# Compact copies of the second half's weights, and a new order of steps at the opening of the first attention

## The reference

```python
def first_block(...):            # two layers; what the change touches is in layer 0
    cq, ckv, kr = z[..., :256], z[..., 256:384], z[..., 384:416]      # z = h @ w_in
    q  = (rmsnorm(cq, q_norm_g) @ w_uq).reshape(b, t, 8, 96)
    kv = (rmsnorm(ckv, kv_norm_g) @ w_ukv).reshape(b, t, 8, 128)
    # q and k normed per head, rotated; softmax attention; retention beside it; @ w_out
    # modulation: 6 chunks per layer of silu(c) @ ada_w + ada_b

def second_block(...):
    x = x + hybrid_mixer(rmsnorm_2(x), w_in, ..., w_out)              # w_in_2: 1024 x 3080
    x = x + memory_cross_attention(rmsnorm_2(x), rmsnorm_2(mem), wq, wkv, wo)
    x = x + peer_ffn(rmsnorm_2(x), wq, subkeys, u_tab, v_tab)
    # peer_ffn: per token 8 heads x 16 experts; rows u_tab[i], v_tab[i] of 1024 floats
    # act = gelu(u_tab[i] . x) * gate;  out = sum act * v_tab[i]
    return rmsnorm_2(x, norm_final_w)
```

## Time and profile before

| | us |
|---|---|
| median of 3 runs | 4487.05 |
| lowest and highest run | 4479.52, 4492.16 |
| profiled execution | 4478.17 |
| its span, first to last instruction | 4476.4 |
| PE busy / DVE busy / POOL busy / ACT busy | 3652.3 / 2022.0 / 1399.2 / 1008.0 |
| bytes moved by DMA | 821.56 MB |

### The profile page before, as it was taken

The page is one execution under the profiler, slowest core; times in us unless marked ns, Lnnn a source line. Parts: engine busy times, 40 slices in busy tenths (PEclk is TensorE's granted clock), DMA queues, the critical chain, the costliest instruction groups (busy, mean ns, idle before and its releaser), DMA issues.

```text
span 4476.4 us, 45304 instructions
## 1 busy us (share of the span) xinstructions
PE 3652.3 (82%) x16837; PEld 2077.9 (46%) x16837; DVE 2022.0 (45%) x4634; ACT 1008.0 (23%) x2265; POOL 1399.2 (31%) x1494
## 2 busy tenths in 40 slices
PE   6788998999999778999997979867777776565555
PEld 3355534555555565444466867434544433111111
DVE  2565062633222583111125324586755655665553
ACT  3564022200000211100025122344132212112111
POOL 0000001162422000000000002656556677776776
PEclk8899999999999899999998989888888888776667
DMA  4232102222222123422211134988889999998998
GB/s 176 76 113 81 57 23 49 76 108 95 76 82 112 64 112 123 153 76 75 75 66 71 57 132 161 351 319 309 284 296 368 346 392 334 350 353 326 354 354 318
DMA packets 287765, 821.56 MB, mean 184 GB/s; under 512 B 24040, under 2 KB 60340, under 8 KB 284244
## 3 DMA queue, kind: packets, MB, share of 16 engines
q0 software_dynamic: 150832, 565.17, 34.2%
q1 hardware_dynamic: 136320, 253.22, 15.9%
q10 hardware_dynamic: 420, 0.62, 0.1%
HBM read 791.67 MB, written 27.26 MB: 183 GB/s over the span
## 4 chain that ended last, share of the span: by engine, by line
PE 57%; DVE 13%; POOL 8%; issue 8%; ACT 5%; DMA 4%; another core or an unknown queue 3%; SPq 0%; DVEq 0%; ACTq 0%; POOLq 0%
PE bank L722 25%; PE bank L2619 6%; PE bank L2855 5%; POOL arena L1170 4%; POOL ring L1161 4%; PE bank L2422 3%; PE bank L2579 2%; PE bank L2474 2%; DVE ring L2279 2%; DMA arena<-in_peer_v,arena 2%; PE bank L2338 1%; PE bank L587 1%; PE bank L2414 1%; PE bank L2559 1%
## 5 line engine op out<-in xcount | busy, mean ns | idle before, releaser
L1161 POOL DMA_INDIRECT ring<-in_peer_u,arena x512 | 569.3, 1112 | 1412.5 <-DVE arena L2226 1071.9
L2855 PE MATMUL bank<-arena 64*64 64x512 f32 x4096 | 697.8, 773 | 375.1 <-issue 311.9
L2279 DVE SCALAR_TENSOR_TENSOR ring<-ring,xT 128x1024 f32<-128x1024 f32 x512 | 614.2, 1222 | 265.7 <-DMA ring<-in_peer_u,arena 244.1
L1170 POOL DMA_INDIRECT arena<-in_peer_v,arena x512 | 579.5, 1132 | 206.2 <-issue 145.1
L722 PE MATMUL bank<-hT,ring 128*128 128x512 f32 (+1 forms) x1536 | 553.3, 522 | 5.1 <-ACT hT L637 5.1
L2855 PEld LDWEIGHTS bank<-arena 64*64 64x64 f32 x4096 | 187.8, 162 | 793.7 <-issue 790.9
L722 PE MATMUL bank<-arena,ring 128*128 128x512 f32 (+1 forms) x1536 | 551.3, 521 | 0.0
L722 PEld LDWEIGHTS bank<-hT,ring 128*128 128x128 f32 x1536 | 292.6, 191 | 264.1 <-issue 250.9
L722 PEld LDWEIGHTS bank<-arena,ring 128*128 128x128 f32 x1536 | 291.8, 190 | 258.1 <-issue 244.2
L2619 PE MATMUL bank<-hT,ring 128*128 128x256 f32 x1536 | 366.7, 398 | 33.6 <-DMA ring<-in_peer_wq 15.6
L2619 PEld LDWEIGHTS bank<-hT,ring 128*128 128x128 f32 x1536 | 302.6, 200 | 125.5 <-issue 54.1
(11 more groups left out here) (520 smaller groups left out, 4581.2 us busy)
## 6 DMA issues: line engine op xcount, KB each, us to landing
ring<-in_mlp_w SPq DMA_DIRECT2D x32, 2048.0 KB, 8.3
ring<-in_ada_w SPq DMA_DIRECT2D x24, 2048.0 KB, 13.0
s_store<-arena POOLq DMA_DIRECT2D x8, 2816.0 KB, 9.6
ring<-in_w_in SPq DMA_DIRECT2D x10, 2048.0 KB, 8.1
arena<-s_store SPq DMA_DIRECT2D x16, 1024.0 KB, 6.9
ring<-in_w_in SPq DMA_DIRECT2D x12, 1024.0 KB
ring<-in_w_out SPq DMA_DIRECT2D x4, 2048.0 KB, 8.0
ring<-in_s_w_glu SPq DMA_DIRECT2D x4, 2048.0 KB, 14.2
```

Source lines behind the costliest of these rows:

```text
L1161: pool.indirect_dma_start(u_row[k % ERING], None, I["peer_u_2"][0], bass.IndirectOffsetOnAxis(idxs[:, k // EXPERTS, k % EXPERTS:k % EXPERT ...
L1170: pool.indirect_dma_start(v_row[v % ERING], None, I["peer_v_2"][0], bass.IndirectOffsetOnAxis(idxs[:, v // EXPERTS, v % EXPERTS:v % EXPERT ...
L2279: dve.scalar_tensor_tensor(row, row, 1.0, h_tok[k // EXPERTS % 2], ALU.mult, ALU.mult, accum_out=dots[k // AGROUP % 2][:, k % AGROUP:k % A ...
L2855: last = pe.matmul(banks[2 * r + n][QUADS[r if y == 0 else 1 - r], :], diag[QUADS[r], s, :], v_row[s][QUADS[r], 512 * n:512 * n + 512], st ...
```

## The change

Three things:

- During the first attention's end, behind the retention blocks, SP issues 32 copies from the weight inputs to a new scratch tensor `weights_kept` in device memory. Each copy takes the 256 columns that one block of the second half needs, so that a partition's share of a block lies in one piece of 8 KB. The second half's loads (`mix1`, `w2_1`, `xq1`, `wo1`, `pq1`) read from there (`kept_blocks`), after a wait of SP for all copies. The first half's loads stay.
- The opening computes z in the order keys, queries 0, queries 1, rotary part. The sums of the key norm come behind queries 0. ACT and DVE follow the same order.
- The six modulation units of the first attention each come one head earlier: the first before head 0's rotation.

```diff
@@ mla_order
     yield "proj", 0
-    for step in ("nsum", "norm", "rot"):
-        for j in range(2):
+    for step in ("nsum", "ada", "norm", "rot"):
+        for j in range(1 if step == "ada" else 2):
             yield step, j
+    yield "adarow", 0
     for n in range(6 * H_A + 3):
         if n < 6 * H_A:
             yield "scores", n
+        if n == 0:
+            yield "adacol", 0
...
-        if h <= ADA_IN_MLA and n % 6 in (2, 3, 4):
-            yield ("ada", "adarow", "adacol")[n % 6 - 2], h - 1
+        if h < ADA_IN_MLA and n % 6 in (2, 3, 4):
+            yield ("ada", "adarow", "adacol")[n % 6 - 2], h
+
+MLA_IN_ORDER = (("z_kv", 2), ("z_q0", 0), ("z_q1", 1), ("z_kr", 3))
@@ build
+        TAIL_WEIGHTS = [*[("w_in_2", (2056, 2568, 0, 512, 1024, 1536)[j // 2] + 256 * (j % 2)) for j in range(12)],
+                        *[(name, 256 * j) for name, n in (("w_out_2", 4), ("xattn_wq_2", 4), ("xattn_wo_2", 4), ("peer_wq_2", 8)) for j in range(n)]]
+        tail_at = {"mix1": 0, "w2_1": 12, "xq1": 16, "wo1": 20, "pq1": 24}
+        weights_kept = nc.dram_tensor("weights_kept", (len(TAIL_WEIGHTS), P, KD * 256), F32).ap()
@@ SP
             for j in range(4):
                 load_block(sp, block0["w_in_r"] + j, w_in_v[:, :, MLA_IN + j * RET_W:MLA_IN + (j + 1) * RET_W])
+            for b, (name, a) in enumerate(TAIL_WEIGHTS):
+                sp.dma_start(weights_kept[b].rearrange("p (k n) -> p k n", k=KD),
+                             I[name][0].rearrange("(k p) n -> p k n", p=P)[:, :, a:a + 256]).then_inc(S("weights_kept"), 16)
             for j in range(2):
                 load_block(sp, block0["w_out"] + j, ...)
...
+            def kept_blocks(name, lo, hi):
+                for j in range(lo, hi):
+                    load_block(sp, block0[name] + j, weights_kept[tail_at[name] + j])
...
-            mix_blocks(1, 0, 3)
+            sp.wait_ge(S("weights_kept"), 16 * len(TAIL_WEIGHTS))
+            kept_blocks("mix1", 0, 3)
...
-            tail_blocks(1, "w2_1", "w_out_2", 256)
-            tail_blocks(1, "xq1", "xattn_wq_2", 256)
+            kept_blocks("w2_1", 0, 4)
+            kept_blocks("xq1", 0, 4)
@@ ACT (DVE and PE likewise)
-            for m in range(4):
+            for name, m in MLA_IN_ORDER:
...
+                if name == "z_q0":
+                    norm_roots(act, "ckv", TBS, KV_LORA, rs=rstd_qk[:, 0, :])
             norm_roots(act, "cq", TBS, Q_LORA)
-            norm_roots(act, "ckv", TBS, KV_LORA, rs=rstd_qk[:, 0, :])
```

More of the change, by code:

```diff
@@ L300 @@
     ("ada_first1", 2),
-    ("z_q", 4), ("z_kv", 2), ("z_kr", 2),
-    ("norm_cq", 2), ("norm_ckv", 2),
+    ("z_kv", 2), ("z_q0", 2), ("norm_ckv", 2),
+    ("z_q1", 2), ("z_kr", 2), ("norm_cq", 2),
     ("v_tok", 6),
@@ L1003, in _, with mix_blocks @@
             MIX_AT = (2056, 2568, 0, 512, 1024, 1536)
-            def mix_blocks(h, lo, hi):
+            def mix_blocks(lo, hi):
                 for j in range(lo, hi):
-                    a, n = (MIX_AT[j], 512) if h == 0 else (MIX_AT[j // 2] + 256 * (j % 2), 256)
-                    load_block(sp, block0[f"mix{h}"] + j, w_in2[:, :, a:a + n])
+                    load_block(sp, block0["mix0"] + j, w_in2[:, :, MIX_AT[j]:MIX_AT[j] + 512])
+            def kept_blocks(name, lo, hi):
+                for j in range(lo, hi):
+                    load_block(sp, block0[name] + j, weights_kept[tail_at[name] + j])
             def mask_loads(h):
@@ L1012, in mask_loads, with tail_blocks @@
                     sp.dma_start(mask(h, j), cst(name)).then_inc(S("g_masks"), 16)
-            def tail_blocks(h, name, src, width, lo=0, hi=None):
+            def tail_blocks(name, src, lo=0, hi=None):
                 w = I[src][0].rearrange("(k p) n -> p k n", p=P)
[L1016 to L1020, removed]
+                for j in range(lo, hi or w.shape[2] // 512):
+                    load_block(sp, block0[name] + j, w[:, :, j * 512:(j + 1) * 512])
+            mix_blocks(0, 2)
+            mix_blocks(2, 3)
             for n in range(8):
@@ L1023, in _ @@
             mask_loads(0)
-            mix_blocks(0, 3, 6)
-            tail_blocks(0, "xkv", "xattn_wkv_2", 512)
-            tail_blocks(0, "w2_0", "w_out_2", 512)
+            mix_blocks(3, 6)
+            tail_blocks("xkv", "xattn_wkv_2")
+            tail_blocks("w2_0", "w_out_2")
             for n in range(8):
@@ L1054, in _ @@
             sp.dma_start(ring[:, 3, :], kv_kept).then_inc(S("kv_moved"), 16)
-            tail_blocks(1, "wo1", "xattn_wo_2", 256)
+            kept_blocks("wo1", 0, 4)
             for n in range(8):
                 filled(sp, ticket0[f"xout1_{n}"])
-            tail_blocks(1, "pq1", "peer_wq_2", 256)
+            kept_blocks("pq1", 0, 8)
             for T_ in range(NTL):
@@ L1200, in _ @@
             norm_shift(act, "l0a", TBS, hT, shift_of(0, 0))
-            for m in range(4):
+            for name, m in MLA_IN_ORDER:
                 for b, (lo, hi) in enumerate(TBS):
-                    t = ticket0["z_q"] + 2 * m + b
+                    t = ticket0[name] + b
                     bank = filled(act, t)
@@ L2339, in _ @@
                     fill(last, t)
+                if name == "z_q0":
+                    norm_sums(pe, "ckv", TBS, prob, 1, per=2)
             norm_sums(pe, "cq", TBS, sqs, 2, per=2)
-            norm_sums(pe, "ckv", TBS, prob, 1, per=2)
             wv = block(pe, block0["ukv"], 1, n=1024)[:, 0, :].rearrange("p (h two v) -> p h two v", h=H_A, two=2)
```

14 lines of the change are left out of this document (7 added, 7 removed).

## The result

The changed kernel took **4439.52 us** (median of 4 runs, 4435.46 to 4445.42) against 4483.28 us for the kernel before (4 runs, 4478.08 to 4492.16): ratio 0.9903, 95% interval 0.9885 to 0.9922. The forecast was 4,449 us with a range of 4,412 to 4,480, and "faster" at 0.74. One execution of e3 took 5627.97 us and is left out of its ratio; the other eleven took 4482.46 to 4495.70.

A forecast was written before the change was run, and what follows sets the result against it. PE was taken to set the pace for 25 of 40 slices, then the gather stage with DMA 80 to 100% busy. Terms -12.6 - 0.4 - 0 - 25 = -38 us from 4,487.05 gave 4,449 us, range 4,412 to 4,480.

The forecast's parts named there:

- 1. Opening order: First attention's opening: `v_tok` starts without a wait at 99.97, first attention product at about 107.9 instead of 120.48; -12.6 us.
- It moves as a whole: Everything behind the first attention product is a chain through ACT and DVE that moves earlier with it, by 12.6 us.
- 2. Modulation unit: First attention: the 3.63 us unit fits PE's 8.71 us wait behind head 0's sums; taken as -0.4 us.
- 3. The copies: SP's queue from 365 us: 32 copies done by 573, before `w_out` is needed at 704; cost 0.
- 4. The loads: Second half beside the gathers: 8 KB rows land a block in about 5.5 us instead of 16; -25 us.
- The others vanish: PE's block waits in the second half: longest, 15.6 us, shrinks by about 10.5; those of 6.7, 6.3, 4.2 vanish.
- term 1: The new order of z products and norms in the first attention's opening, put at -12.6 us.
- What is next late: Gather stage, once weight loads land sooner: the DVE product on its gather is the next to be late.
- A: Gather stage is limited by bytes, large rows don't help, only the opening counts: 4,474 us; chance 0.22.
- D: Second half: large rows hold up gathers, 32 blocks each stalling the ticks by 3 us: 4,542 us; chance 0.05.
- C: Copies run into retention and delay `w_out`; at 80 GB/s it is 97 us late: 4,546 us; chance 0.06.
- B: The mixed stage's whole chain speeds up as sooner landings free the next slots; -55, 4,419 us; chance 0.15.

The follow-up runs named there:

- e3: Kernel before plus the 32 copies, which nobody reads; second half's loads still in 1 KB rows, old order: 4487.9 us, ratio 1.0001 to the kernel before.
- e7: Kernel before with only the new order of z products and norms; modulation units at old places, no copies: 4477.34 us, ratio 0.9971.
- e1: Changed kernel without the copies and with the old 1 KB row loads, so only the new opening and modulation order: 4476.03 us, ratio 0.9972.
- e10: The changed kernel once more, unaltered, with more runs, against the kernel before: 4434.07 us, ratio 0.9907.
- e8: Kernel before with only the modulation units moved to their new places: 4471.6 us, ratio 0.9996.
- e9: Whole change with every copy made four times (128 copies), against the kernel before: 4453.57 us, ratio 1.0178.
- e2: Kernel before plus the copies and the second half's loads in 8 KB rows, opening and modulation in old order: 4465.75 us, ratio 0.9955.
- e6: Kernel before without copies, old order, second half's blocks read in 8 KB rows from the u table: 4361.16 us, ratio 0.9952.
- e4: Whole change with the compact 1 MB blocks stored and read in 1 KB rows, against the kernel before: ratio 0.9984.
- e5: Whole change with each block in 4 KB rows (two pieces, 64 copies of 512 KB), against the kernel before: ratio 0.9928.

## Why the prediction was right

*1. Opening order (-12.6).* Right, in place and size. `v_tok` began at 99.32 (said: 99.97), the first attention product at 107.39 (said: 107.9), 13.1 us earlier; e7 measured -13.0 and e1 -12.6 us at the end. "It moves as a whole" held from there to the rotation (-12.0) and to `w_out` (706.88 against 717.48: -10.6; e10 has 705.79 and e1 703.91, e7 705.47).

*2. Modulation unit (-0.4).* Right within what can be measured: e8 -1.8 us, interval -7.6 to +4.5. The gap closed as worked out, 8.71 = 3.63 + 5.10 to 0.02 us.

*3. The copies (0).* Right: e3 1.0001. The time at which `w_out` is needed was read from the long row (704 instead of 682), which cost nothing here. The rate was mis-sized, on the safe side. I took the 161 GB/s of a spill and an end by 573 us; SP's next load was issued at 472.54, and with a landing of 13.1 us, the median of the last copies in the page, they were through by some 485 us, where the DMA share falls from 1.01 to 0.17 (from 480 to 485 us and from 485 to 490): 33.6 MB in 120 us, 280 GB/s. In e9, 134.2 MB in 434 us make 309 GB/s.
The Trainium skill (DMA: Bandwidth & Descriptors, Latency and other measured facts) gives 207 GB/s for copies at a 512 KiB pitch, by which, an estimate, they would have lasted 162 us. These copies, whose source rows are 1 KB long, were faster than that; the measurement decides.

*4. The loads (-25).* Right in kind, its size in the middle of what was measured: -20 in the old order (e2, e6), -29 to -30 on top of the new opening (e1 to the whole). Three steps in it were off. The landing of a block was put at 5.5 us where the earlier trace rows had 16 to 18; the kept blocks in the chains took 4.8 to 8.8 us, with a median of 8.4 in e9. "The others vanish" failed in one place: two waits stayed, 6.1 us before the mixer's product at 2817.98 and 6.6 before the `peer_wq` products at 3548.73, 12.7 in all where I had left 5. And I counted the waits as the trace of before had them, 32.8 us (34.6 with one of 1.8 that I hadn't counted), though term 1 moves the whole stage and one wait was short by luck of its place. That makes up for the two steps before it, so that the size of the term came out this near is in part luck. The sum of -38 stood against -43.5 and -41.6.

Of the signs named, the idle time by DMA fell to 12.7 us in the profiled execution and to 8.7 in e10 (said: under 10). The stage from 2,770 to 3,660 us was said to be 25 us shorter; it was 12.8 us shorter between the two traces and 28 between e3 and e2.

*What is next late.* Said: the DVE product on its gather. In the mixed stage (2,770 to 3,660 us) that wait rose, but little: groups of DVE and POOL after, against 25.6 and 177.3 us in the earlier trace rows.

```profile
L2297 DVE SCALAR_TENSOR_TENSOR ring<-ring,xT 128x1024 f32<-128x1024 f32 x257 | 307.0, 1220 | 39.8 <-DMA ring<-in_peer_u,arena 30.0 <-issue 8.6
...
L1178 POOL DMA_INDIRECT ring<-in_peer_u,arena x252 | 289.5, 1149 | 240.6 <-DVE ring L2297 177.7 <-issue 62.9
```

*The rivals.* A (bytes are the limit) fell: the same bytes came in 20 us less with the large rows alone (e2, e6), at 362 GB/s in the stage with loads where e3 on the same chip had 339. D would show in DVE's wait, +4.4 us here, not 96. C waits at about three times the copies; e9 had four. B (-55) promised more than the waits held.
*The stage behind.* I said that it would stay as long. It took 815.2 us instead of 824.1. But it took 814.2 us in e1 too, whose loads are the old ones, and 820.5 in e2: this is scatter between executions, not the change.

## What to carry to other kernels

How soon a load lands beside a stream of gathers depends here on the length of its rows, at the same bytes: make the rows of a late weight at least as long as the stream's, and if the tensor's layout doesn't allow it, copy it in an idle stretch of the DMA, where it was free to within 6 us, as long as nothing that is queued behind it became late. Rows of 4 KB, the gathers' own size, had most of the gain here. Size the gain from all waits that the change can reach, and when another part of the change moves the stage in time, treat each short wait in it as one that may be long in the new place; two parts of a change may then bring more (or less) than each alone.

## What was unexpected of the hardware

- Copies within device memory with source rows of 1 KB ran at 280 to 309 GB/s beside a PE that was 93% busy and showed no loss (102.14 of 110 us busy against 100.95). From the spill's 161 GB/s I had expected little more than half of that.
- A DMA share is not a rate: with loads in 1 KB rows had 349 GB/s at 0.94, with 8 KB rows it was 362. At a share of 1.02 to 1.03 stand 326 GB/s (copies in e9), 334 (copies in the trace of after), 380 (e1) and 397. Here "94% busy" was no proof that bytes were the limit.
- The same kernel differs between chips by more than the whole change is worth: the kernel before took 4488.10, 4380.87 and 4477.18 us. The stage of gathers alone took 752 and 760 us in e4 and e5 on the second chip and 813 to 815 us in e1, after and e10, while the second half's first kept load was issued at the same time (2765.62 in e5, 2765.79 in e10). The mixed stage took 826.5 us in e5 and 848.2 in e10. What differs in that chip stays open; no run here looked at it.
